# A fused transformer block: query projection in three chunks of four heads instead of four of three, and the modulation steps spread between the attention units

## What is computed

```python
m = silu(cond) @ w_mod + b_mod            # six vectors of 2048 for each condition: shift, scale, gate, twice
h = rms_norm(x, g_attn) * (1 + sc1) + sh1
z = h @ w_in                              # columns of three head groups
# A: 6 query heads, 2 key/value heads; B: the same, windowed, with a sink logit; C: 4 latent heads (MLA)
q, k = rope(rms_norm(z_q, gain)), rope(rms_norm(z_k, gain))      # context tokens: no rope
o = softmax(q @ k.T * scale) @ v          # per head; latent tokens also read 128 cached keys
x1 = x + g1 * (concat(o_A, o_B, o_C) @ w_o)
h2 = rms_norm(x1, g_ffn) * (1 + sc2) + sh2
y = x1 + g2 * moe(h2)                     # 32 experts, top 2 of one group of 8
```

## Time and profile before

| | before |
|---|---|
| median of three runs | 1730.23 us (1730.15 to 1730.38) |
| the profiled execution, its own time | 1730.17 us |
| its span, first to last instruction | 1728.3 us |
| PE busy | 1619.3 us, 94% |
| DVE, ACT, POOL busy | 619.3, 265.4, 99.0 us |
| mean granted clock of PE | 0.98 of full |
| DMA | 581.93 MB, mean 337 GB/s |

### The profile page before, as it was taken

One profiled execution on the slowest core, in us unless ns is written; L12 is line 12 of the kernel. 1 busy time (PEld: TensorE's weight loads), 2 busy tenths in 40 slices (PEclk: granted clock), 3 DMA queues, 4 the chain that ended last, 5 costly groups with the idle time before them and its releaser, 6 DMA issues.

```text
span 1728.3 us, 18419 instructions
## 1 busy us (share of the span) xinstructions
PE 1619.3 (94%) x6799; PEld 661.0 (38%) x6844; DVE 619.3 (36%) x1333; ACT 265.4 (15%) x709; POOL 99.0 (6%) x189
## 2 busy tenths in 40 slices
PE   5999999999989999999999999999899989988998
PEld 2445545544433444444323332332333233233332
DVE  3112222102226201352443454444444443544444
ACT  2003221102224100011011101101110110111010
POOL 1022100101011100000000000000000000000000
PEclk8999999999999999999999999999999999999999
DMA  9994671755569722189999999999999999999995
GB/s 369 384 342 195 250 270 62 281 211 205 227 225 374 316 97 97 60 331 425 425 429 427 427 429 426 425 428 424 425 428 425 428 425 427 426 426 427 416 428 223
DMA packets 92639, 581.93 MB, mean 337 GB/s; under 512 B 9110, under 2 KB 24310, under 8 KB 55390
## 3 DMA queue, kind: packets, MB, share of 16 engines
q1 hardware_dynamic: 84944, 554.20, 78.9%
q0 software_dynamic: 5920, 22.61, 3.5%
q10 hardware_dynamic: 1728, 4.51, 0.7%
HBM read 584.04 MB, written 7.05 MB: 342 GB/s over the span
## 4 chain that ended last, share of the span: by engine, by line
PE 71%; DMA 15%; DVE 2%; issue 2%; ACT 1%; SPq 0%; ACTq 0%
PE bank L1226 24%; DMA ring<-in_w 15%; PE bank L974 13%; PE bank L1076 10%; PE bank L1136 7%; PE bank L871 3%; PE bank L1258 2%; PE bank L1061 2%; PE bank L1185 2%; PE bank L1273 1%; PE bank L1208 1%; PE bank L1122 1%; PE bank L1036 1%; PE bank L1044 1%; PE bank L1011 1%
## 5 line engine op out<-in xcount | busy, mean ns | idle before, releaser
L1226 PE MATMUL bank<-ring,r 128*64 128x512 f32 x1920 | 470.6, 620 | 44.1 <-DMA ring<-in_w 44.1
L1226 PEld LDWEIGHTS bank<-ring,r 128*64 128x64 f32 x1920 | 129.6, 140 | 303.0 <-issue 303.0
L974 PE MATMUL bank<-ring,r 128*128 128x384 f32 (+1 forms) x672 | 243.1, 520 | 0.0
L1916 DVE TENSOR_TENSOR bank<-bank,r 128x512 f32<-128x512 f32 x192 | 134.2, 699 | 278.8 <-PE bank L1136 266.1
L1258 PE MATMUL bank<-ring,mod_row 128*64 128x512 f32 x896 | 196.2, 594 | 8.2 <-ACT mod_row L1472 7.9
L1076 PE MATMUL bank<-ring,r 128*128 128x512 f32 x384 | 169.6, 595 | 0.7 <-issue 0.7
L974 PEld LDWEIGHTS bank<-ring,r 128*128 128x128 f32 x672 | 126.9, 191 | 109.8 <-issue 46.5
L1136 PE MATMUL bank<-r 128*128 128x512 bf16 x495 | 137.6, 382 | 7.2 <-issue 7.2
L1918 DVE TENSOR_TENSOR r<-r,bank 128x512 f32<-128x512 f32 x192 | 131.8, 686 | 6.6
L1258 PEld LDWEIGHTS bank<-ring,mod_row 128*64 128x64 f32 x896 | 75.3, 137 | 119.5 <-issue 109.3
L1076 PEld LDWEIGHTS bank<-ring,r 128*128 128x128 f32 x384 | 71.3, 190 | 82.2 <-issue 82.1
(11 more groups left out here) (270 smaller groups left out, 1201.5 us busy)
## 6 DMA issues: line engine op xcount, KB each, us to landing
ring<-in_w SPq DMA_DIRECT2D x180, 2048.0 KB, 17.5
ring<-in_w_mod SPq DMA_DIRECT2D x96, 1024.0 KB, 13.1
ring<-in_w SPq DMA_DIRECT2D x19, 1024.0 KB, 7.5
ring<-in_w_o SPq DMA_DIRECT2D x16, 1024.0 KB, 11.1
ring<-in_w_in SPq DMA_DIRECT2D x20, 768.0 KB, 6.0
ring<-in_w_in SPq DMA_DIRECT2D x8, 1024.0 KB, 5.3
r<-mod_d POOLq DMA_DIRECT2D x8, 1024.0 KB, 16.8
r<-in_w SPq DMA_DIRECT2D x5, 1024.0 KB, 8.4
```

Source lines behind the costliest of these rows:

```text
L974: mm = pe.matmul(acc[acc_of(a)][:, 0:w], h_t[:, k, t * P:(t + 1) * P], wu[:, j, :], start=(k == 0), stop=(k == KD - 1))
L1226: mm = pe.matmul(ps[64 * c:64 * c + 64, :], xg_t[:, j, 64 * c:64 * c + 64], big_cut(slot_of(u), (8, 512))[:, j % 8, :], start=(j == 0), st ...
L1916: v.tensor_tensor(ps[:, :], ps[:, :], g2b[:, min(t, 1), cols], ALU.mult).then_inc(strip_scaled, 1)
```

## The change

The six query heads of A and the six of B were four chunks of three heads (`aq0`, `aq1`, `bq0`, `bq1`). Now they are three chunks of four: `q0` (A 0 to 3), `q1` (A 4, 5 and B 0, 1) and `q2` (B 2 to 5). The columns of `q1` do not lie together in `w_in`, so its four units are halves in rows and halves in columns, and each matmul reads its 512 columns from two slots. The list has 32 jobs instead of 35. In a job with attention units a `mod` step now stands ahead of each unit instead of all in front. The drain of the C units moves from the job (`aq1`, 1) to behind the job (`q1`, 2), with a `mod` step ahead of each of its pieces. The drain at the end of the A units is no longer made; these units go on into the B units. Rotary embedding of four heads is done as two pieces of two heads. The ring starts at slot 0 instead of 8, as there are 137 units instead of 141 before the experts' weights.

```diff
-          ("aq0", Q_A, 384), ("aq1", Q_A + 384, 384), ("bq0", Q_B, 384),
-          ("akv", K_A, 512), ("bq1", Q_B + 384, 384), ("bkv", K_B, 512)]
+          ("q0", Q_A, 512), ("q1", Q_A + 512, 512), ("akv", K_A, 512), ("q2", Q_B + 256, 512),
+          ("bkv", K_B, 512)]
+Q_KINDS = ("q0", "q1", "q2")
-RING_FROM = 8
+RING_FROM = 0
...
-            attends = (name == "aq0" and t > 0) or (name == "aq1" and t < 2) or name in ("bq1", "bkv")
+            attends = (name == "q0" and t > 0) or (name == "q1" and t < 2) or name in ("q2", "bkv")
             job("proj", (name, t), norm=not attends)
...
-            else:
-                mods(3 if name == "aq0" or (name, t) == ("bq0", 0) else 2)
+            count = 0 if name == "cq1" else 2 if name in ("akv", "bkv") or (name, t) == ("q2", 2) else 3
+            fill = later[:count]
+            del later[:count]
+            if name == "q1" and t == 2:
+                while scored or turned_p:
+                    if fill:
+                        mod(*fill.pop(0))
+                    advance()
+            if not attends:
+                while fill:
+                    mod(*fill.pop(0))
...
-            if name == "aq0" and t:
-                attend("C", [t - 1])
-            if name == "aq1" and t < 2:
-                attend("C", [t + 2], flush=(t == 1))
-            if name == "bq1":
+            if name == "q0" and t:
+                attend("C", [t - 1], fill=fill)
+            if name == "q1" and t < 2:
+                attend("C", [t + 2], fill=fill)
+            if name == "q2":
                 if t == 0:
                     steps.append(("turn", pending.pop(0)))
-                attend("A", range(SHARE), [t])
+                attend("A", range(SHARE), [t], fill)
             if name == "bkv":
-                attend("A", range(SHARE, HEADS_A), [t])
+                attend("A", range(SHARE, HEADS_A), [t], fill)
             if attends:
                 steps.append(("norm", n))
-    while scored or turned_p:
-        advance()
+    advance()
+    mods(1)
     steps.append(("cache", "b"))
-    steps.extend(("turn", n) for n in pending)
+    steps.append(("turn", pending.pop(0)))
+    mods(1)
+    steps.append(("turn", pending.pop(0)))
...
+                    if name == "q1":
+                        for k in range(KD):
+                            m = unit_no[("in", name, k // 8 * 2)]
+                            if k % 8 == 0:
+                                arrived(m)
+                                arrived(m + 1)
+                            at = ring_slot(m)
+                            both = ring[:, at:at + 2, :].rearrange("p s (j n) -> p s j n", j=8)[:, :, k % 8, :]
...
-                            last = rope(z[:, 0:heads * HD].rearrange("p (h x) -> p h x", h=heads), heads, 64,
-                                        *tables(jobs[n][1], ("cos", "sin")))
+                            for i in range(0, len(names), 2):
+                                after(last)
+                                last = rope(z[:, i * HD:(i + 2) * HD].rearrange("p (h x) -> p h x", h=2), 2, 64,
+                                            *tables(jobs[n][1], ("cos", "sin")))
```

More of the change, by code:

```diff
@@ L319, in build @@
     n_pv_c = sum(atts[u][0] == "C" for u in pv_units)
-    pv_bank_from = in_turn.index(jobs.index(("bq1", 0)))
+    pv_bank_from = in_turn.index(jobs.index(("q2", 0)))
     def acc_of(r):
@@ L669, in build @@
                 done = own[:-1]
+                if s[0] == "proj" and jobs[s[1]][0] == "q1":
+                    frees[done.pop()] = (acc_full, acc_uses)
             else:
@@ L967, in _ @@
                     acc_wait(a)
+                    if name == "q1":
+                        for k in range(KD):
[5 more added lines that the diff above has]
+                            both = ring[:, at:at + 2, :].rearrange("p s (j n) -> p s j n", j=8)[:, :, k % 8, :]
+                            mm = pe.matmul(acc[acc_of(a)][:, :].rearrange("q (s n) -> q s n", s=2),
+                                           h_t[:, k, t * P:(t + 1) * P], both, start=(k == 0), stop=(k == KD - 1))
+                            if k == KD - 1:
+                                mm.then_inc(acc_full, 1)
+                            elif t == TILES - 1 and k in (7, 8):
+                                mm.then_inc(slot_free[ring_slot(unit_no[("in", name, k - 7)])], 1)
+                        a += 1
+                        continue
                     for i in range(4):
@@ L1337, in _ @@
                         e.wait_ge(state_out, 16 * states)
-                    if kind in ("aq0", "aq1", "bq0", "bq1"):
-                        heads, w = 3, HD
+                    if kind in Q_KINDS:
+                        heads, w = 4, HD
                     elif kind in ("cq0", "cq1"):
@@ L1369, in _ @@
                     else:
-                        last = e.activation(z[:, 0:384], ps[:, 0:384], ACT.Copy)
+                        last = e.activation(z[:, 0:heads * w], ps[:, 0:heads * w], ACT.Copy)
                     last.then_inc(z_ready, 1)
@@ L1398, in _ @@
                         last = e.activation(dst, ps[:, 0:256].rearrange("p (h x) -> p h x", h=2), ACT.Copy)
-                    elif kind in ("aq0", "aq1", "bq0", "bq1"):
-                        t = jobs[n][1]
-                        h0 = {"aq0": 0, "aq1": 3, "bq0": 6, "bq1": 9}[kind]
-                        last = e.activation(qo[:, t, h0:h0 + 3, :].rearrange("p h x -> p (h x)"), ps[:, 0:384], ACT.Copy)
+                    elif kind in Q_KINDS:
+                        t, h0 = jobs[n][1], 4 * Q_KINDS.index(kind)
+                        last = e.activation(qo[:, t, h0:h0 + 4, :].rearrange("p h x -> p (h x)"), ps[:, :], ACT.Copy)
                     elif kind in ("cq0", "cq1"):
@@ L1729, in scale_by @@
                                                       op0=ALU.mult, op1=ALU.mult)
[L1731 to L1735 removed]
+                    if kind in ("akv", "bkv") + Q_KINDS:
+                        if kind in Q_KINDS:
+                            names = ["a_qn" if 4 * Q_KINDS.index(kind) + i < HEADS_A else "b_qn" for i in range(4)]
+                        else:
+                            names = [kind[0] + "_kn"] * 2
+                        for i, name in enumerate(names):
+                            last = scale_by(z[:, i * HD:(i + 1) * HD], z[:, i * HD:(i + 1) * HD], i, gain_of[name])
                         if jobs[n][1]:
[L1737 to L1739 removed]
+                            for i in range(0, len(names), 2):
+                                after(last)
+                                last = rope(z[:, i * HD:(i + 2) * HD].rearrange("p (h x) -> p h x", h=2), 2, 64,
+                                            *tables(jobs[n][1], ("cos", "sin")))
                     elif kind in ("cq0", "cq1"):
@@ L2039, in _ @@
                     heads, dim = {"ckv": (1, KV_RANK), "cq0": (2, 192), "cq1": (2, 192), "kvc": (2, 192),
-                                  "akv": (2, HD), "bkv": (2, HD)}.get(kind, (3, HD))
+                                  "akv": (2, HD), "bkv": (2, HD)}.get(kind, (4, HD))
                     sv = ss[b][:, 0:heads]
```

16 lines of the change are left out of this document (6 added, 10 removed).

## The result

The changed kernel takes 1735.98 us, the median of seven runs (1733.68 to 1738.89); the kernel before took 1730.15 beside it (1728.84 to 1730.38). The ratio is 1.0035, with a 95% interval of 1.0026 to 1.0044: 6 us slower, outside the forecast range. The profiled execution took 1736.46 us, its span is 1734.5, 6.2 more than before.

What follows compares the result with a forecast made beforehand. PE was taken to bound the mixer and output projection, DMA the experts, whose end moves with the mixer. The terms summed to +0.9 us won from 1730.17, giving 1729.3 us, range 1723 to 1733.

Steps and rivals of the forecast that it cites:

- Cutting the `mod` pieces up: Mixer: 13 more modulation pieces at 0.2 us each for switching; −2.6 us (−1.4 to −3.3).
- the three signs: Wrong if the wait behind (`q1`, 2) is under 3, PE waits for a slot before `q1`, or experts don't move.
- Jobs and turns: Projections: twelve jobs of 10.32 become nine of 13.73, transposes in nine turns instead of twelve; +0.5 us.
- Group read-out: First step of SH2: its 0.90 wait behind G1 goes, as three pieces of a unit stand between; +1.0 us.
- Waits in the A units: Behind (`q2`, 1) three steps cover waits before `pt` and `pv`: +1.1 us; the four two-step groups: 0.
- First A units: They and their steps take 6.4 us: −0.1; the job behind loses its half clock two times in three: +1.1.
- The C drain leaves: Drain of the C units leaves (`aq1`, 1), where it took 5.27 with holes; +2.4 us (2.15 to 2.6).
- The C drain arrives: Drain behind (`q1`, 2): second `pt` waits 5.8 us for VectorE behind the `norm`, half clock costs 2.0; together −7.8.
- The A drain goes: End of the A units: 2.6 of waits and 2.8 of half clock go, the 0.94 wait stays; +5.3 us.
- the first: Rival: the wait behind (`q1`, 2) does not bite, 5.8 and 2.0 stay away; 1721.5 us, chance 0.13.
- the third: Rival: weights of `q1` land late, 1742 us at twice 13.1; chance 0.06, shared with a costly two-slot read.
- The second: Rival: half clock stays after the last and behind the first A units, 2.8 and 1.1 lost; 1733.2 us, chance 0.12.

Runs made afterwards that it cites:

- experiment 8: Changed kernel with only the three chunks of four heads: old step order, old drains, 18 steps left for the B units; 1730.89 us, ratio 1.0006.
- experiment 12: The kernel of experiment 8 with the new end of the A units; 1726.75 us, ratio 0.9981.
- experiment 5: Changed kernel with all modulation steps ahead of a job's units and the `norm` of (`q1`, 2) behind the C drain; 1723.68 us, ratio 0.9959.
- experiment 3: Changed kernel with all modulation steps of a job ahead of its units again, both drains as changed; 1731.65 us, ratio 1.0011.
- experiment 1: Changed kernel with only the `norm` of (`q1`, 2) moved behind the drain of the C units; 1730.43 us, ratio 1.0004.
- Experiment 10: Changed kernel with two modulation steps ahead of a group's first score and any third between the first two scores; 1730.67 us, ratio 1.0002.
- experiment 9: Kernel before with only the steps spread, one ahead of each unit; chunks of three heads and both drains kept; 1732.71 us, ratio 1.0018.
- experiment 6: Kernel before with only the new end of the A units, three steps behind (`bq0`, 0), 16 left for the B units; 1726.63 us, ratio 0.998.
- experiment 7: Kernel before with the new end of the A units, one step behind (`bq0`, 0), 18 left for the B units; 1722.35 us, ratio 0.9961.
- experiment 4: Changed kernel with the edits of experiment 1 and experiment 2 together; 1726.0 us, ratio 0.9977.
- experiment 2: Changed kernel with the turn behind the group's first score in jobs with attention units, except (`q2`, 0) and (`q1`, 2); 1733.8 us, ratio 1.0026.
- experiment 11: Changed kernel with the edits of Experiment 10 and experiment 1 together; 1723.82 us, ratio 0.9964.

## Why the prediction was wrong, step by step

Four of these kernels lead from the one before to the changed one, each a single edit from the next. Beside each step between medians stands what the prediction's terms give for it, in us won.

| step | medians | won | forecast |
|---|---|---|---|
| three chunks (experiment 8) | 1730.15 to 1730.89 | −0.7 | +0.5 |
| new end of the A units (12) | to 1726.75 | +4.1 | +5.3 |
| C drain one job later, norm behind it (5) | to 1723.68 | +3.1 | +2.4 |
| norm in front of the drain (3) | to 1731.65 | −8.0 | −7.8 |
| steps spread between the units | to 1735.98 | −4.3 | −0.6 |
| the dip in the job behind the first A units | in none alone | | +1.1 |
| sum | | −5.8 | +0.9 |

**The step that failed** is *Cutting the `mod` pieces up*, with the sentence on the A units that put the two-step groups at 0. It charged each further piece with 0.2 for switching and asked what a step covers behind the first score. What the steps cover ahead of the first score was not asked: ACT's queue, where the copies of the turn stand behind the eviction of the job that has just ended. Only at (`q2`, 0) was that wait worked out (0.9; the trace has 0.95). It stands at nine group heads, 5.8 us of it unforeseen, while the group terms were −2.6 + 1.0 + 1.1 − 0.1 = −0.6. In the profiles at full clock, spreading the steps makes the four C groups 4.8 us longer (experiment 1 against 5) and the four A groups with two steps 2.0 longer, and takes 1.9 off the other two A groups (the changed kernel against experiment 3): 4.9 in all, for the medians' 4.3. A small part of it is the price of a piece: two further pieces in a later C group cost 0.66 beside the wait of 0.89 (12.02 against 10.47), 0.33 each and not 0.2.

That is 3.7 of the 6.7 us by which the forecast missed. How much falls to this step depends on the order in which the edits are made: with the norm behind the drain, spreading the steps costs 6.8 in the medians (experiment 5 to 1), and then the norm in front costs 5.5. Experiment 10, which covers the first scores and leaves the third step between them, wins 5.3, and experiment 9 shows the same loss with three heads (2.6). The remaining 3 us lie in terms that are each off by 1.2 or less, where single medians of these kernels can't settle more.

None of the three signs by which the prediction would know that it was wrong came up: the wait was over 3, PE waited for no slot ahead of `q1`, and the experts' part moved with the mixer. They watched the terms that were worked out, and the failed one had been put at nothing. What did differ is that the B units start 3.7 us later (524.50 against 520.83) and not 1 us earlier.

The other terms, in its own order:

- *Jobs and turns* (+0.5): jobs of 13.73 as forecast, and the chunks alone between 0.5 faster and 2.6 slower.
- *Group read-out* (+1.0): the 0.90 of the earlier trace rows is gone when the steps are spread and is back as 0.91 in experiment 3.
- *Waits in the A units*: (`q2`, 1) takes 6.60 with no wait, against 7.43 with the steps in front: +0.8 for a forecast +1.1.
- *First A units*: 6.26 for a forecast 6.4. The job behind ran at full clock, as forecast; but it did so in experiments 5 to 8 and 12 too, where the holes of before (0.56 and 0.84) are still there, and in experiment 3 it took 15.59. So the reason given, that steps cut the holes up, isn't shown.
- *The C drain leaves* (+2.4): its old place is 5.2 us shorter and its new one 3.6 longer at full clock (experiments 12 and 5), 1.6 won; the medians say 3.1.
- *The C drain arrives* (−7.8): the wait of 5.8 was measured at 5.69 and the clock's 2.0 at 1.83. Undone, 5.5 us come back in the medians with the steps spread, 8.0 with the steps in front. The queue of VectorE was read rightly from the order and two dissimilar rows. The twelve rotary instructions take 2.8 us from 331.53 to the copy at 334.34, with 0.29 shown for one; they overlap, as the row of before said. The trace therefore does not agree with the sentence of the Trainium skill that the prediction weighed ("VectorE: DVE Perf Modes", section "The DRAIN you can't avoid"), that the next instruction does not start until the pipe is empty; the same section adds that an instruction that is not held starts earlier, which the prediction left out.
- *The A drain goes* (+5.3): 5.5 in the profile of experiment 7. In the changed kernel the `pt` at 520.18 is 4.32 from the first B score, forecast 4.4.
- *What passes through*: the mixer's end moved by 6.07 and the span by 6.2.
- *What bounds the kernel*: the mixer reaches beyond slice 12, and in slice 13, the B units, DMA is at 9 tenths in the earlier trace rows. This changed nothing, as PE waits for no weight there.

Of the rivals, the first (the new wait doesn't bite) and the third (`q1` late) are refuted: the wait is there, and no wait for a weight stands ahead of a `q1` job. The second (old dips stay) didn't come true either: dips did turn up, but in the C groups and not at the two places that it named. The times nearest to the result were those of the third and the second, 1733.7 and 1733.2, and neither for its reason.

## What to carry to other kernels

When fill work is spread between units, first ask of the *first* unit in each group what its cover was for. Here a turn and one step, 1.5 us, stood where ACT needed 2.1, and nine of ten groups waited, two of them with a dip behind the wait; a second step repaired it. Fill work is also a store that must last: two steps spent too early left the last two units without any, which cost some 4 us. Work on an in-order queue ahead of a copy that frees a bank (here a `norm` that nobody needed yet) is best moved behind it.

## What the runs showed of the hardware

The same holes, 0.89 and 0.43 us in a C group, were followed by half clock (1.67 for a `mod` step, 0.50 to 0.75 granted) in one execution and by full clock (1.04) in another. Such dips also come where nothing was changed. Some 180 us behind the start of the output projection PE waits 0.41 and then 0.69 or 0.70 in every one of the 14 profiles; the group of matmuls behind these waits runs at full clock in eight of them and partly at half in six (experiments 1, 3, 4, 8, 9 and 12; 0.50 granted in its first 2 us in experiment 8). In the kernel before and in experiment 1:

```profile
757.73 3.68 PE L948 MATMUL bank<-r,cst 128*128 128x512 f32 x8
755.46 5.38 PE L966 MATMUL bank<-r,cst 128*128 128x512 f32 x8
```

In these six, and in experiment 2 without this dip, the part from the output projection to the end takes 1157.6 to 1159.1 us; in the others 1156.2 to 1156.7. The last `pv` of the B units takes 3.5 to 3.9 instead of 2.2 in experiments 1, 5, 6 and 10, behind the same wait of 0.58 as elsewhere.

Between runs the time spread over 1 to 3.4 us in experiments 3, 5, 7 and 10, and over 4 to 7.4 us in the others (experiments 5, 7 and 11 have only five runs). Which holes decide this isn't settled: experiments 3 and 10 are among the steady ones and have the wait of 5.7. A single profile with or without a dip therefore says little about what a change does to the clock.
